# A hybrid GLA and SSD layer with a mixture of experts on one core: the first weights' high part, one modulation block and the scan's pairwise products each moved ahead of their neighbour

## What is computed

```python
mod = c_act @ ada_w[l] + ada_b[l]                  # c_act = silu(c), six vectors of 1024
h = rms_norm(x, norm1_g[l]) * (1.0 + sc1) + sh1
proj = h @ w_in[l]
q, k, v, g_out, gk_low, z, xbc, dt_raw, gates = split_cols(proj, IN_SIZES)
# GLA, chunks of 64 tokens
update = jnp.einsum('bclhk,bclhv->cbhkv', k_dec, v)
state = decay * prev + update
o = jnp.einsum('bclhk,cbhkv->bclhv', q, state)
# SSD, chunks of 64 tokens
l_mask = jnp.exp(-jnp.abs(seg))
cb = jnp.einsum('bctgn,bcsgn->bctsg', c_m, b_m)    # the pairwise products
y_diag = jnp.einsum('bctsg,bctsgr,bcsgrp->bctgrp', cb, l_mask, xdt)
# then gates, two output projections, residual, norm, 32 experts (top 2), residual, norm
```

## Time and profile before

| | |
|---|---|
| median of 3 runs | 727.92 us |
| the profiled execution | 727.88 us |
| its span, first to last instruction | 726.1 us |
| PE busy | 682.2 us (94%) |
| DVE busy | 399.6 us (55%) |
| ACT busy | 263.8 us (36%) |
| mean granted PE clock | 0.977 of full |

### The profile page before, as it was taken

The page is one execution under the profiler, slowest core; times in us unless marked ns, Lnnn a source line. Parts: engine busy times, 40 slices in busy tenths (PEclk is TensorE's granted clock), DMA queues, the critical chain, the costliest instruction groups (busy, mean ns, idle before and its releaser), DMA issues.

```text
span 726.1 us, 13249 instructions
## 1 busy us (share of the span) xinstructions
PE 682.2 (94%) x5650; PEld 548.8 (76%) x5650; DVE 399.6 (55%) x685; ACT 263.8 (36%) x371; POOL 70.7 (10%) x69
## 2 busy tenths in 40 slices
PE   7879899999998699999999999999999999999893
PEld 7869799989876477789998999866666666665441
DVE  4536676759975646997877456571523222222225
ACT  2325644544777044344545243232122112112003
POOL 0001000000000260440000000000111111111111
PEclk9999999999999599999999999999999999999998
DMA  8965587767535035333657836998999999999992
GB/s 365 422 249 173 211 310 294 288 235 269 195 116 174 0 117 174 123 117 126 235 220 267 312 135 252 383 351 317 420 407 402 419 419 421 419 420 418 419 367 95
DMA packets 31053, 200.74 MB, mean 276 GB/s; under 512 B 5031, under 2 KB 5415, under 8 KB 7826
## 3 DMA queue, kind: packets, MB, share of 16 engines
q1 hardware_dynamic: 27378, 193.27, 69.1%
q0 software_dynamic: 3616, 6.62, 2.4%
HBM read 194.83 MB, written 10.75 MB: 283 GB/s over the span
## 4 chain that ended last, share of the span: by engine, by line
PE 79%; DVE 7%; DMA 5%; ACT 4%; issue 3%; SPq 2%; DVEq 0%; POOL 0%; ACTq 0%; POOLq 0%
PE ps L1526 77%; DMA ring<-in_expert_pieces 4%; ACT ring_rounded L623 2%; SPq L454 2%; DVE ring_rounded L907 2%; DMA ring<-in_pieces 1%; PE ps L1645 1%; PE ps L1942 1%; DVE r_lm L1084 1%; DVE r_lm L1020 1%; DVE r_lm L1057 0%; DVE r_kq L1146 0%; DVE r_xs_rounded L1202 0%; ACT r_lm L695 0%; ACT r_lm L694 0%
## 5 line engine op out<-in xcount | busy, mean ns | idle before, releaser
L907 DVE TENSOR_TENSOR ring_rounded<-ring,ring_rounded 128x2048 fp32r<-128x2048 f32 x60 | 137.8, 2303 | 71.8 <-ACT ring_rounded L623 71.4
L1526 PE MATMUL ps<-hT_rounded,ring_rounded 128*128 128x256 f32 x832 | 151.6, 289 | 12.2 <-ACT ring_rounded L623 8.9
L1526 PEld LDWEIGHTS ps<-hT_rounded,ring_rounded 128*128 128x128 f32 x832 | 130.5, 195 | 16.6 <-ACT ring_rounded L623 9.3
L623 ACT CAST ring_rounded<-ring 128x2048 fp32r<-128x2048 f32 x60 | 114.0, 1904 | 41.3 <-PE ps L1526 27.9
L1526 PE MATMUL ps<-ring_rounded,hT_rounded 128*128 128x512 f32 x352 | 111.8, 399 | 0.0
L1526 PE MATMUL ps<-x_sb_rounded,ring_rounded 128*128 128x256 f32 x416 | 110.3, 286 | 0.0
L1526 PEld LDWEIGHTS ps<-x_sb_rounded,ring_rounded 128*128 128x128 f32 x416 | 77.6, 194 | 1.1 <-issue 0.2
L1526 PEld LDWEIGHTS ps<-ring_rounded,hT_rounded 128*128 128x128 f32 x352 | 65.6, 192 | 14.2 <-issue 1.7
L582 POOL DMA_INDIRECT y_rows<-r_st,r_btm x29 | 28.5, 983 | 347.3 <-DVE r_st L1409 347.3
L1526 PE MATMUL ps<-ring,r_lm 128*64 128x256 f32 x512 | 59.6, 380 | 1.2 <-DMA ring<-in_expert_pieces 1.2
L831 ACT ACTIVATE sq<-ps 128x128 f32<-128x128 f32 x32 | 8.9, 278 | 141.7 <-PE ps L1526 141.7
(11 more groups left out here) (327 smaller groups left out, 996.7 us busy)
## 6 DMA issues: line engine op xcount, KB each, us to landing
ring<-in_pieces SPq DMA_DIRECT2D x74, 1024.0 KB, 5.2
ring<-in_expert_pieces SPq DMA_DIRECT2D x48, 1024.0 KB, 16.1
r_z<-in_expert_pieces SPq DMA_DIRECT2D x12, 1024.0 KB, 11.8
r_xs<-in_expert_pieces SPq DMA_DIRECT2D x12, 1024.0 KB, 13.7
g_sb<-in_expert_pieces SPq DMA_DIRECT2D x6, 1024.0 KB
r_st<-in_expert_pieces SPq DMA_DIRECT2D x6, 1024.0 KB
r_bt<-in_expert_pieces SPq DMA_DIRECT2D x6, 1024.0 KB
hT<-in_expert_pieces SPq DMA_DIRECT2D x6, 1024.0 KB, 16.8
```

The costliest lines, as they stand in the source:

```text
L623: nc.scalar.copy(high_of(p_), slot_of(p_)).then_inc(hi_ok, 1)
L907: nc.vector.tensor_tensor(low_of(p_), slot_of(p_), high_of(p_).bitcast(F32), ALU.subtract).then_inc(lo_ok, 1)
L1526: return nc.tensor.matmul(o, l, r, start=start, stop=stop)
```

## The change

It moves work within the streams of PE, ACT and DVE and adds two small things, a one-column square root on ACT and four products of ones on PE:

```diff
-PLAN += [("unit", "g", 1), ("cb", 0), ("cb", 1)] + [("gU", c, hp) for c in range(NC) for hp in range(2)]
+PLAN += [("cb", 0), ("cb", 1), ("unit", "g", 1)] + [("gU", c, hp) for c in range(NC) for hp in range(2)]
...
             link(nc.scalar.activation(col("c", 0, 8), col("c", 0, 8), ACT.Silu))
+            act.wait_ge(s_ones, 1)
+            link(nc.scalar.activation(norm_s[:, 0:1], ones[:, 0:1], ACT.Sqrt))
             mix_taken(act, "sumsq")
             nc.scalar.activation(norm_s, norm_m, ACT.Sqrt).then_inc(x_sqrt, 1)
+            split_to(1)
             for q in range(QUARTERS):
...
+                    if u == ("z", 0) and half == 0:
+                        gla_updates(1)
...
             modulation(("quarter", 0))
-            keep_clock(12)
+            keep_clock(16)
             products_of_start(("pair", 0, 0, 0), 0).then_inc(start_read, 1)
             modulation(("quarter", 1))
             products_of_start(("rest", 0, 0, 0), 0)
             products_of_start(("rest", 0, 0, 0), 1).then_inc(start_read, 1)
+            modulation(("quarter", 2))
             products_of_start(("pair", 1, 0, 0), 1).then_inc(start_read, 1)
-            modulation(("quarter", 2))
             products_of_start(("pair", 2, 0, 0), 2).then_inc(start_read, 1)
...
             rows_of_sums(1)
-            project(("g", 1))
             pe.wait_ge(silu_done, 16)
             for t in range(TT):
                 bank = begin(("cb", t))
...
+            project(("g", 1))
...
-            for t in range(TT):
-                gla_updates(t)
+            gla_updates(0)
```

## The result

| | before | changed |
|---|---|---|
| median, 4 runs each | 728.21 us | 706.32 us (706.09 to 706.91) |
| ratio | | 0.9702, 95% interval 0.9685 to 0.9718 |
| span of the profiled execution | 726.1 us | 704.5 us |
| PE busy | 94% | 96% |

The account below looks back on a forecast made before the run. The prediction took PE, busy nearly all the time, as the bound, so only its waits and slow clock could be won. 727.88 less 10.0 (start) and 13.6 (middle) gave 704.3 us, range 701.9 to 708.8.

Parts of the forecast that it names:

- Table load, cast, first product: Start: table load hidden (1.3 us), cast ahead of h, PE's first weight product at 17.3 instead of 20.30, 3.0 us earlier.
- Clock behind the short gap: Start: PE's gap of 1.2 us instead of 5.14 leaves the clock at 2.4 GHz for the first products, gain 1.6 us.
- Third modulation: Start, ahead of `pair 2`: PE's wait of 3.75 us goes, and 1.65 us of half clock behind it.
- rival 2: Start: early transfers become the bound, through a late `pair 0` or modulations waiting for pieces; 706.5 to 709 us, chance 10%.
- Start in all: Sum of the start's gains, 3.0 + 1.6 + 3.75 + 1.65 = 10.0 us, bounds 8.0 to 10.5.
- Middle: Decay sums to end of `z 0`: waits of 7.34 and 2.5 us go, new 1.0 us wait, full clock; gain 13.6 us.
- Behind: After the middle: GpSimd's scan block moves less than PE but stays ahead; the gain carries through whole.
- Expert stage: Near the DMA's limit; its stream starts 23.6 us sooner and ends so much sooner, with the same length.
- Rival 1: Clock: no fall at `xbc 1` 702.6 us; another at a new short gap 706.0; low from the 1.0 us gap 709, 4%.

Follow-up runs that it names:

- the kernel without the root: The changed kernel without the one-column square root, so the table load stands in the norm's chain again; 708.14 us, ratio 0.9743.
- The experiment with the held block: The changed kernel with GpSimd's second block held until DVE scaled the GLA outputs (705.41 us) or, in a second kernel, took the first SSD states (704.55 us).
- The middle alone: The kernel before with only the middle's edits: the place in `PLAN`, the pairwise products, the second updates; 716.24 us, ratio 0.9842.
- no early cast: The changed kernel with the first weight cast put back behind h's high parts; 708.65 us, ratio 0.9752.
- both mends: The changed kernel with pairwise products between the last gate unit's halves and GpSimd's second block held until DVE took the first SSD states; 704.15 us, ratio 0.9671.

## Why the prediction was right, and what was off

Predicted 704.3 us (701.9 to 708.8), measured 706.32. The direction, the places and the mechanisms of the gains hold. The 2.0 us are three misses, at the start, in the middle and behind it, less 0.5 us that came back without having been forecast.

- *Table load, cast, first product.* Forecast at 17.3, came at 17.67. The load's 1.3 us were right (1.30 by the kernel without the root), the cast fitted (the piece was there at 13.5, I had taken 14.2 from even spacing). PE finished the sum of squares 0.35 us later than before, as ACT's 11.28 shows against the 10.91 of the earlier trace rows; among the kernels here that moment moved between 10.5 and 11.3 us. A term of the start has that much play.
- *Clock behind the short gap.* Right: 1.00 over 16 to 22 us. The pair gained 7.20 - 5.78 = 1.4 us (forecast 1.6). The third product of the pair is due at 17.3 + 3.8 = 21.1 and not at 21.0 as the forecast says; it came at 21.49, and DVE's subtraction, begun at 18.96, was done at about 21.2.
- *Third modulation.* Forecast 5.4 us, 5.37 in the trace between the second and the fourth modulation, 5.40 when undone. PE waited for no transfer (rival 2).
- *Start in all.* Forecast 10.0, measured 53.98 - 44.56 = 9.4.
- *Middle.* Wait for M's product gone, second wait gone, new wait 0.97 (forecast 1.0), all right. The span from the last decay sum to the outputs fell from 42.77 to 29.78, by 13.0 us instead of 13.6; the term mis-sized is the time of each block at full clock: updates 2.00 and not 1.9, a half of `z 0` 5.6 and not 5.5, `g 1` 11.1 and not 11.0.
- *Behind.* "GpSimd's block moves less than PE but stays ahead" is the step that failed. It stays ahead of PE, but it now lies across the norm of the outputs on DVE. Counted from the last decay sum, the outputs came 13.0 us sooner (42.77 before, 29.78 after), but GpSimd's block only 6.5 us (250.21 - 219.20 = 31.0 before, 234.28 - 209.74 = 24.5 after). This cost 1.35 us. I had also looked only for what waits for GpSimd and not for what shares the time with it. The experiment with the held block settles the cause. The trace of the kernel before had a sign of it, a GpSimd product of three times its usual length beside a subtraction on DVE:

```profile
252.22 2.31 DVE L907 TENSOR_TENSOR ring_rounded<-ring,ring_rounded 128x2048 fp32r<-128x2048 f32 x1
252.33 3.10 POOL L575 TENSOR_TENSOR r_xs<-r_xs,par 128x512 f32<-128x512 f32 x1
255.39 1.04 POOL L572 TENSOR_TENSOR r_v<-r_xs,dtb 128x512 f32<-128x512 f32 x1
```

- *Expert stage.* Right: from `z 2` to the end 447.4 us before and 446.9 after, at the same 419 to 420 GB/s between 600 and 640 us. Where in this stretch the 0.5 us came back is open; that they made the forecast look better is luck.
- *Sum of the misses.* 0.6 + 0.6 + 1.35 - 0.5 = 2.05 us. The forecast's lower end, 701.9, is 0.2 below the 702.1 that its own sum gives, which changes nothing here.
- *Rival 1.* The clock fell behind the `xbc 1` wait in this run as well, so neither of its figures was tested by the changed kernel. The middle alone had the case without a fall: behind a wait of 3.35 us the clock stayed at 1.00, and from the product behind the wait to the products with `r_lm` it took 87.61 - 81.78 = 5.83 us, against 87.46 - 80.16 = 7.30 before. A fall there costs 1.5 us, where the rival had 1.7. Before, and then in the middle alone:

```profile
80.16 0.36 PE L1526 MATMUL ps<-hT_rounded,ring_rounded 128*128 128x256 f32 x1 [3.36 <-DVE ring_rounded L907]
...
87.46 1.04 PE L1645 MATMUL ps<-par,r_lm 128*128 128x128 f32 x8
```

```profile
81.78 0.35 PE L1526 MATMUL ps<-hT_rounded,ring_rounded 128*128 128x256 f32 x1 [3.35 <-DVE ring_rounded L907]
...
87.61 1.04 PE L1647 MATMUL ps<-par,r_lm 128*128 128x128 f32 x8
```

## What to carry to other kernels

A wait on the pacing engine is priced with the slow clock behind it: here the waits that went or shrank, less the new ones, make 15.2 us (3.84 + 3.75 + 7.34 + 2.46 - 0.97 - 1.25), and PE's busy time, which holds the half clock behind them, fell by 6.3 us more. When a block is moved, ask of every engine whose work moves by another amount what it now lies beside, not only whether it is still in time. A result that waits for a chain of other engines can be started ahead of an independent unit, or, better by 1.08 us here, between that unit's two halves, where the chain has cover on both sides.

## What the runs showed of the hardware

- DVE's small steps, 128x8 elements at 0.17 us each, took 0.90 to 0.97 us when GpSimd was in one of its 128x512 products of 1.04 us, and ended with it; in the other direction a GpSimd product took 3.02 to 3.10 us beside DVE's subtractions of about 2.3 us. The Trainium skill ("SBUF — State Buffer", SBUF: two separate sides) says that the two engines share a pair of ports as an exclusive lock, held for a whole instruction, which a VectorE operation with two SBUF inputs, or in a mode that uses two ports, also needs against GpSimd. The trace agrees for the steps with two inputs; in which mode the step L893 ran, with its one input and 0.90 us, no run here shows. The price is not in proportion to the work: the twelve steps took 6.6 us instead of 2.4, 4.2 us more in all.
- The granted clock fell behind gaps of PE of 2.31 us (no early cast), 3.14, 3.74, 4.90 and 7.35 us, and not behind 0.97, 1.30 and 2.40 us. The length of the gap alone does not decide: ahead of `xbc 1` it fell behind a gap of 1.87 us in the kernel with both mends, and it did not behind one of 3.35 us in the middle alone, with PE busy at 1.00 ahead of both. In the kernel with both mends, and in four others, it also fell without any gap, behind 3.7 us of products with 48 columns. The changed kernel runs the same work there at 1.00. With both mends, the window behind those products, the wait ahead of `xbc 1` and a window behind it:

```profile
61.50:65.00 3.50, 3.50 (x18) 3.50 (x18) 3.02 (x10) 2.72 (x6) 0.00 (x0) 0.51 0.93 323
```

```profile
70.67 0.35 PE L1531 MATMUL ps<-hT_rounded,ring_rounded 128*128 128x256 f32 x1 [1.87 <-DVE ring_rounded L912]
```

```profile
72.00:75.00 3.00, 3.00 (x16) 3.00 (x15) 3.00 (x5) 1.16 (x1) 0.00 (x0) 0.50 0.34 142
```

The fall at 61.5 us cost little, because PE waits for DVE behind it, and that wait shrank from 3.4 to 1.9 us. What sets the moment of a fall is not shown by these runs.
